# Sums of the latent heads in two bank pairs, value blocks inside the attention's first steps, front reordered, modulation rows turned by transposes

## The chip, the cores and the metric

The kernel is one program on one core of a Trainium2 chip. TensorE (PE) multiplies, VectorE (DVE), ScalarE (ACT) and GpSimd (POOL) work element by element, SyncE (SP) issues the transfers. The metric is the device time of one execution in microseconds; lower is better.

## The reference

Two transformer blocks of depth 2 run over 512 latent tokens (the first block also over 256 context tokens), width 1024. What matters here is the first layer of the first block:

```python
shift, scale, gate = modulation(c, ada_w[i], ada_b[i])      # silu(cond) @ ada_w + ada_b, for c and c_ctx
h = rms_norm(x, norm_g[i]) * (1 + scale) + shift
lat = split_cols(jnp.dot(h, w_in), EVEN_SPLITS)
q = jnp.dot(rms_norm(q_lat, q_norm), w_uq).reshape(bsz, n, A_HEADS, A_QK)       # 8 heads of 96
kv = jnp.dot(rms_norm(kv_lat, kv_norm), w_ukv).reshape(bsz, n, A_HEADS, A_NOPE + A_V)
q = rms_norm(q, q_gain)
k = rms_norm(k, k_gain)                                     # then a rotation of 32 of the 96 rows
a_x = block_attention(q_x, jnp.concatenate([k_x, k_c], axis=1), jnp.concatenate([v_x, v_c], axis=1), scale)
```

Beside this attention the layer has a gated linear attention ("gla") whose output is also normalized per head. The later layers are not touched, except that their modulation vectors are made by the same helper.

## The kernel before, in words

Each engine has its own hand-written instruction list; semaphores alone order them. Tokens lie along the free axis (768 = 512 + 256), so a result of 768 columns takes two PSUM banks. PSUM has 8 banks of 512 floats.

The front: SP issues `cond`, `vec`, the tokens and then the weights. `Modulation` k (twelve of them, classes START_MOD, GLA_MOD and LATE_MOD) multiplies the conditioning rows with four weight tiles (`pe`, L320), ACT copies the result out of PSUM (`copied`, L329), PE turns it into columns (`turned`, L336), DVE adds the bias (`added`, L343). DVE multiplies the tokens with the norm factor (L2816), makes the gains (L2806), ACT shifts and rounds (L2658, L2662), DVE takes the remainder (L2829). The first three weight tiles are split into a rounded part by ACT (`first_hi`, L522) and a remainder by POOL (`first_lo`, L527); `first_pe(t, h)` (L539 to L541) multiplies half h of tile t, four chunks of six matmuls.

The latent stage (class Latent): PE projects six query tiles (`q_tile`, L1118) and four key tiles (`k_tile`, L1134). For each of 20 heads (4 gla outputs, 8 query heads, 8 key heads) ACT squares (L1235), PE sums over the partitions into banks 4 and 5 (`sums`, L1154), ACT takes the logarithm out of PSUM (L1249) and the exponential (L1251), and DVE multiplies (`normed`, L1354). Query heads are also rotated (POOL L1347, DVE L1359, L1362), key heads are first taken from PSUM (DVE L1380). `sums(n)` waits on `hd_log` n, that is until ACT has read the sums of head n-1 out of the one pair of banks. Six value blocks (`value`, L1166, evicted by ACT L1305) follow among the last three heads' sums, into banks 0 to 3.

Then `att_mla` (class Pairs) runs its 24 steps: scores (L1929, banks 0 to 3), DVE maxima (L2028), ACT exponentials (L1994), PE turnings of the probabilities (L1942, banks 4 and 5), copies (L2003, L2049), values (L1956, bank 6). No engine begins it before all heads and all six value blocks are done (`latent.wait`).

## Time and profile before

| | us |
|---|---|
| median of 3 runs | 2326.94 |
| lowest, highest | 2325.99, 2331.77 |
| profiled execution | 2324.17 |
| its span in the profile | 2322.1 |
| PE busy | 2245.8 |
| DVE busy | 1144.2 |
| ACT busy | 981.6 |
| POOL busy | 371.4 |

The span is the part of the execution that the profile sees. PE is by far the busiest engine, so what moves the time is its idle time, the time in which it runs at the lower clock, and the instructions it executes.

### The profile page before, as it was taken

The page shows a single profiled execution, that of the slowest core. Times are in us where ns is not written, and L with a number is a line of the kernel's source. Part 1 is how long each engine was busy: PE and PEld are TensorE (multiplying, and loading weights), DVE is VectorE, ACT ScalarE, POOL GpSimd, SP SyncE. Part 2 cuts the span into 40 slices and gives each one's busy share as a digit, 9 for nine tenths or more (in the row PEclk, how much of TensorE's full clock was granted, in tenths as well). Part 3 has the DMA queues.
Part 4 walks back from the last instruction along what each step waited for, and adds up shares of the span by engine and source line. Part 5 has one row for each costly group of instructions (what it writes and reads, how often), then busy time and mean ns, then how long its engine had stood idle before and what let it go on. Part 6 is the DMA issues. An engine that isn't in the chain of part 4 may idle for free.

```text
span 2322.1 us, 32240 instructions
## 1 busy us (share of the span) xinstructions
PE 2245.8 (97%) x12310; PEld 1753.9 (76%) x12310; DVE 1144.2 (49%) x1778; ACT 981.6 (42%) x1642; POOL 371.4 (16%) x247
## 2 busy tenths in 40 slices
PE   6999999899999999999999999999999999999998
PEld 4888775366878877777876788888888667888886
DVE  5000453544353303754556476674555654766645
ACT  5121435645245524654256443342342764333422
POOL 2233001100323331030000300004300012000143
PEclk9999999899999999999999999999999999999999
DMA  8122241200132222124510323333344103333331
GB/s 328 46 64 64 82 168 25 76 34 1 47 117 73 66 80 78 56 85 118 141 55 4 97 91 94 97 90 100 93 130 131 37 23 96 91 96 94 92 99 46
DMA packets 58429, 197.72 MB, mean 85 GB/s; under 512 B 8059, under 2 KB 8443, under 8 KB 58044
## 3 DMA queue, kind: packets, MB, share of 16 engines
q1 hardware_dynamic: 58300, 195.94, 27.1%
q8 instruction: 89, 1.46, 0.2%
q14 instruction: 40, 0.33, 0.0%
HBM read 184.04 MB, written 2.10 MB: 80 GB/s over the span
## 4 chain that ended last, share of the span: by engine, by line
PE 89%; ACT 5%; DVE 4%; issue 1%; DMA 0%; POOL 0%; SPq 0%; DVEq 0%; ACTq 0%; POOLq 0%
PE PS L660 7%; PE PS L658 7%; PE PS L659 7%; PE PS L1929 4%; PE PS L2618 4%; PE PS L2620 3%; PE PS L2619 3%; PE PS L1956 3%; PE PS L1597 3%; PE PS L1942 3%; PE PS L610 3%; PE PS L611 3%; PE PS L609 3%; PE PS L854 2%; PE PS L856 2%; PE PS L855 2%
## 5 line engine op out<-in xcount | busy, mean ns | idle before, releaser
L658 PE MATMUL PS<-H_HI,W_SPLIT 128*128 128x512 f32 x672 | 265.5, 395 | 0.0
L660 PE MATMUL PS<-H_HI,W_SPLIT 128*128 128x512 f32 x672 | 264.9, 394 | 0.0
L659 PE MATMUL PS<-H_LO,W_SPLIT 128*128 128x512 f32 x672 | 264.5, 394 | 0.0
L504 POOL TENSOR_TENSOR W_SPLIT<-WT,W_SPLIT 128x1024 fp32r<-128x1024 f32 x43 | 104.6, 2434 | 612.8 <-ACT W_SPLIT L493 495.5
L470 ACT ACTIVATE W_SPLIT<-WT 128x1024 fp32r<-128x1024 f32 x80 | 84.8, 1060 | 267.3 <-PE PS L660 267.3
L2969 DVE TENSOR_TENSOR W_SPLIT<-WT,W_SPLIT 128x1024 fp32r<-128x1024 f32 x80 | 98.0, 1225 | 150.1 <-ACT W_SPLIT L470 150.0
L1062 POOL TENSOR_TENSOR OUT_HALF<-WT,OUT_HALF 128x512 fp32r<-128x512 f32 x48 | 71.3, 1487 | 610.0 <-ACT OUT_HALF L1020 610.0
L2955 DVE TENSOR_TENSOR G_LO<-SB,G_HI 128x512 fp32r<-128x512 f32 x43 | 100.4, 2335 | 109.0 <-ACT G_HI L2777 109.0
L659 PEld LDWEIGHTS PS<-H_LO,W_SPLIT 128*128 128x128 f32 x672 | 126.0, 188 | 30.4 <-issue 0.5
L658 PEld LDWEIGHTS PS<-H_HI,W_SPLIT 128*128 128x128 f32 x672 | 126.2, 188 | 29.9 <-issue 0.5
L660 PEld LDWEIGHTS PS<-H_HI,W_SPLIT 128*128 128x128 f32 x672 | 126.2, 188 | 29.8
L2618 PE MATMUL PS<-G_HI,W_SPLIT 128*128 128x512 f32 x344 | 135.7, 394 | 0.2
L2620 PE MATMUL PS<-G_HI,W_SPLIT 128*128 128x512 f32 x344 | 134.9, 392 | 0.0
L2619 PE MATMUL PS<-G_LO,W_SPLIT 128*128 128x512 f32 x344 | 133.5, 388 | 0.0
L611 PE MATMUL PS<-HN_HI,W_HALF 128*128 128x512 f32 x352 | 118.7, 337 | 0.0
L610 PE MATMUL PS<-HN_LO,W_HALF 128*128 128x512 f32 x352 | 118.7, 337 | 0.0
L609 PE MATMUL PS<-HN_HI,W_HALF 128*128 128x512 f32 x352 | 118.5, 337 | 0.0
L2039 DVE CUSTOM_DVE_ANT_0 SB<-PS,SB 128x512 f32<-128x512 f32 (+3 forms) x160 | 78.7, 527 | 68.9 <-PE PS L1929 65.5
L1805 POOL TENSOR_TENSOR W_HALF<-WT,W_HALF 128x512 fp32r<-128x512 f32 x60 | 82.5, 1376 | 164.4 <-ACT W_HALF L1634 164.4
L929 DVE TENSOR_TENSOR W_SPLIT<-WT,W_SPLIT 128x1024 fp32r<-128x1024 f32 x42 | 51.5, 1225 | 115.2 <-ACT W_SPLIT L891 115.2
L891 ACT ACTIVATE W_SPLIT<-WT 128x1024 fp32r<-128x1024 f32 x42 | 44.5, 1060 | 146.1 <-PE PS L856 98.7
L1942 PEld LDWEIGHTS PS<-SB 128*128 128x128 f32 x640 | 70.6, 142 | 45.3 <-issue 34.3
(353 smaller groups left out, 5257.9 us busy)
## 6 DMA issues: line engine op xcount, KB each, us to landing
WT<-weights SPq DMA_DIRECT2D x313, 512.0 KB, 3.6
SB<-SB SPq DMA_DIRECT2D x128, 64.0 KB
SB<-weights SPq DMA_DIRECT2D x13, 512.0 KB, 13.0
XT<-tokens SPq DMA_DIRECT2D x4, 768.0 KB, 7.2
SB<-rpb SPq DMA_DIRECT2D x8, 384.0 KB, 3.6
HT<-rpb SPq DMA_DIRECT2D x8, 384.0 KB, 3.7
out<-HT SPq DMA_DIRECT2D x4, 512.0 KB, 3.2
SB<-late SPq DMA_DIRECT2D x1, 1280.0 KB, 5.9
```

What stands on the lines that cost most here:

```text
L504: g.tensor_tensor(w[:, 1, :], W[:, (g0 + t) % SLOTS, :], w[:, 0, :].bitcast(F32), ALU.subtract).then_inc(sem("w_lo"), 1)
L609: pe.matmul(dst, hi, HN_HI[:, c, at:end], start=(c == 0), stop=False)
L610: pe.matmul(dst, hi, HN_LO[:, c, at:end], start=False, stop=False)
L611: last = pe.matmul(dst, lo, HN_HI[:, c, at:end], start=False, stop=(c == KC - 1))
L658: pe.matmul(PS[:, s, :], hi, H_HI[:, c, :], start=(c == 0), stop=False)
L659: pe.matmul(PS[:, s, :], hi, H_LO[:, c, :], start=False, stop=False)
L660: last = pe.matmul(PS[:, s, :], lo, H_HI[:, c, :], start=False, stop=(c == KC - 1))
L1942: last = pe.transpose(PS[:, 4 + k % 2, (b - b0) * 128:(b - b0) * 128 + 128], self.p(s, b // nb)[:, (b % nb) * 128:(b % nb) * 128 + 128], I ...
L2618: pe.matmul(PS[:, n, :], hi, ghi, start=first, stop=False)
L2619: pe.matmul(PS[:, n, :], hi, glo, start=False, stop=False)
L2620: last = pe.matmul(PS[:, n, :], lo, ghi, start=False, stop=(u == FC - 1))
L2955: v.tensor_tensor(lo, G[:, t, :], hi.bitcast(F32), ALU.subtract).then_inc(sem("g_lo"), 1)
```

## The change

- Sums: heads 4 to 19 use banks 4, 5 and 6, 7 in turn (`sum_bank`). `sums(n)` then waits for the logarithm of head n-2, not n-1.
- Values: blocks 0 to 2 follow the attention's first scores, blocks 3 to 5 the first step's turnings; they use banks 4 to 7. Their six evictions, and ACT's first split of the next weights (`window.out_hi`), move into ACT's first two attention steps. PE begins scores 0 without waiting for the value blocks.
- Modulation: `turned` is four transposes (128x128) in place of four matmuls with a 2-column selection; `added` is a sum over the four row groups out of PSUM and then the bias add. The identity matrix is loaded by itself between `vec` and the tokens.
- Front: remainders of tiles 1 and 2 are made by DVE, between its norm products; ACT splits the first half of tile 2 earlier; PE puts one chunk of tile 1 between the last modulation and its turning.

```diff
                 for b in range(4):
-                    last = pe.matmul(PS[:, self.turned_bank, 2 * b:2 * b + 2], self.row[:, b * 128:b * 128 + 128],
-                                     SB[:, vec_at + VEC["sel"]:vec_at + VEC["sel"] + 2], start=True, stop=True)
+                    last = pe.transpose(PS[:, self.turned_bank, 128 * b:128 * b + 128], self.row[:, b * 128:b * 128 + 128], IDENT)
...
-                v.tensor_tensor(MOD[:, self.chunk:self.chunk + 4, :], PS[:, self.turned_bank, 0:8].rearrange("p (c s) -> p c s", s=2),
-                                SB[:, at:at + 4].unsqueeze(2).broadcast_to([128, 4, 2]), ALU.add).then_inc(sem("mod_added"), 1)
+                mod = MOD[:, self.chunk:self.chunk + 4, :]
+                v.tensor_reduce(mod, PS[:, self.turned_bank, :].rearrange("p (c g s) -> p c s g", g=4, s=32)[:, :, 0:2, :], AX.X, ALU.add)\
+                 .then_inc(sem("mod_summed"), 1)
+                v.wait_ge(sem("mod_summed"), self.k + 1)
+                v.tensor_tensor(mod, mod, SB[:, at:at + 4].unsqueeze(2).broadcast_to([128, 4, 2]), ALU.add).then_inc(sem("mod_added"), 1)
...
+            def sum_bank(self, n):
+
+                return 6 if n >= 4 and n % 2 else 4
+
             def sums(self, pe, n):
                 _, parts, _ = self.head(n)
                 pe.wait_ge(sem("hd_squared"), n + 1)
-                if n >= 1:
+                if n == 5:
+                    pe.wait_ge(sem("kv_log"), 2)
+                elif n >= 6:
+                    pe.wait_ge(sem("hd_log"), n - 1)
+                elif n >= 1:
                     pe.wait_ge(sem("hd_log"), n)
...
+            def first_values(self, pe, att):
+
+                pe.wait_ge(sem("k_out"), 8)
+                pe.wait_ge(sem("hd_done"), 2)
+                pe.wait_ge(sem("hd_normed"), 14)
+                att.scores(pe, 0)
+                for b in range(3):
+                    self.value(pe, b)
+
+            def late_values(self, pe):
+                for b in range(3, 6):
+                    self.value(pe, b)
+
+            def values_out(self, act, s):
+
+                if s < 2:
+                    for b in range(3 * s, 3 * s + 3):
+                        self.value_out(act, b)
+                if s == 1:
+                    window.out_hi(act, 0, 0)
+                    window.out_hi(act, 0, 1)
...
             sp.dma_start(SB[:, vec_at:vec_at + NVEC], vec).then_inc(sem("vec_in"), 16)
+            sp.dma_start(IDENT, con[:, 0:128]).then_inc(sem("vec_in"), 16)
...
             START_MOD[2].turned(pe)
             START_MOD[3].pe(pe)
+            first_pe(pe, 1, 0, [0])
             START_MOD[3].turned(pe)
-            first_pe(pe, 1, 0)
+            first_pe(pe, 1, 0, [1, 2, 3])
             first_pe(pe, 2, 0)
...
                     v.tensor_tensor(H[:, c, :], X[:, c, :], RS0, ALU.mult).then_inc(sem("normed"), 1)
-                START_MOD[2 * part].added(v)
+                    if c == 5:
+                        START_MOD[2].added(v)
+                        v.wait_ge(sem("half_lo"), 2)
+                        first_lo(v, 1, 0)
+                        first_lo(v, 1, 1)
+                if part:
+                    first_lo(v, 2, 0)
+                else:
+                    START_MOD[0].added(v)
```

The first place is PE's front, from the last modulation on (L320 is its multiplication, L336 the turning, L539 to L541 and in the changed kernel L542 to L544 the first tiles). Before:

```order
L320 MATMUL PS<-WT,SB 32x512 [waits w_ready7]
L320 MATMUL PS<-WT,SB 32x512
L336 MATMUL PS<-SB 128x2 [waits mod_added,ada_copied]
L336 MATMUL PS<-SB 128x2 x3
L539 MATMUL PS<-HN_HI,W_FIRST 128x512 [waits half_lo]
```

The same place of the changed kernel:

```order
L320 MATMUL PS<-WT,SB 32x512 [waits w_ready7]
L320 MATMUL PS<-WT,SB 32x512
L542 MATMUL PS<-HN_HI,W_FIRST 128x512 [waits half_lo]
L543 MATMUL PS<-HN_LO,W_FIRST 128x512
L544 MATMUL PS<-HN_HI,W_FIRST 128x512
L542 MATMUL PS<-HN_HI,W_FIRST 128x256
L543 MATMUL PS<-HN_LO,W_FIRST 128x256
L544 MATMUL PS<-HN_HI,W_FIRST 128x256
L336 MATMUL PS<-SB 128x128 [waits mod_added,ada_copied]
L336 MATMUL PS<-SB 128x128 x3
```

One chunk now stands ahead of the turning, and the turning is four transposes.

The second place is DVE's front, the second half of the norm products (L2859 in the changed kernel; L529 is the remainder, L343 the sum out of PSUM, L346 the bias, L2849 the gain):

```order
L2859 TENSOR_TENSOR HT<-XT,SB 128x768 x2
L343 TENSOR_REDUCE SB<-PS 128x8 [waits ada_turned]
L346 TENSOR_TENSOR SB<-SB 128x8 [waits mod_summed]
L529 TENSOR_TENSOR W_FIRST<-SB,W_FIRST 128x512 [waits half_hi,half_lo]
L529 TENSOR_TENSOR W_FIRST<-SB,W_FIRST 128x512 [waits half_hi]
L2859 TENSOR_TENSOR HT<-XT,SB 128x768 x2
L529 TENSOR_TENSOR W_FIRST<-SB,W_FIRST 128x512 [waits half_hi]
L343 TENSOR_REDUCE SB<-PS 128x8 [waits ada_turned]
L346 TENSOR_TENSOR SB<-SB 128x8 [waits mod_summed]
L2849 SCALAR_TENSOR_TENSOR SB<-SB 128x8 [waits mod_added]
L529 TENSOR_TENSOR W_FIRST<-SB,W_FIRST 128x512 [waits half_hi]
```

Before, four norm products stood together, then both bias adds and the gain, and the four remainders were POOL's.

The third place is PE's end of the latent stage (L1154 sums, L1166 a value block, L1929 scores). Before, from the value blocks after the last sums on:

```order
L1166 MATMUL PS<-WT,SB 128x512 x4
L1166 MATMUL PS<-WT,SB 128x512 [waits v_out1]
L1166 MATMUL PS<-WT,SB 128x512
L1166 MATMUL PS<-WT,SB 128x512 [waits v_out1]
L1166 MATMUL PS<-WT,SB 128x512
L1929 MATMUL PS<-SB,HT 128x256 [waits v_out1,hd_normed,hd_done]
L1929 MATMUL PS<-SB,HT 128x256
L1929 MATMUL PS<-SB,HT 128x512 x2
L1929 MATMUL PS<-SB,HT 128x256 [waits at_exped] x2
```

The changed kernel (L1169 sums, L1187 a value block, L1963 scores), from the last sums on:

```order
L1169 MATMUL PS<-SB 96x512 [waits hd_log,hd_squared]
L1169 MATMUL PS<-SB 96x256
L1963 MATMUL PS<-SB,HT 128x256 [waits hd_normed,hd_done,k_out]
L1963 MATMUL PS<-SB,HT 128x256
L1963 MATMUL PS<-SB,HT 128x512 x2
L1187 MATMUL PS<-WT,SB 128x512 [waits hd_log,w_ready6]
L1187 MATMUL PS<-WT,SB 128x512 x3
L1187 MATMUL PS<-WT,SB 128x512 [waits hd_log]
L1187 MATMUL PS<-WT,SB 128x512
L1963 MATMUL PS<-SB,HT 128x256 [waits at_exped,hd_normed,hd_done]
```

The first scores moved ahead of the value blocks, and three blocks stand between the scores of steps 0 and 1; the other three (not shown) stand behind the first step's turnings.

## Rows read from the trace of the kernel before

**Rows 1.** The page, busy time, share of the span and instructions of each engine.

```profile
PE 2245.8 (97%) x12310; PEld 1753.9 (76%) x12310; DVE 1144.2 (49%) x1778; ACT 981.6 (42%) x1642; POOL 371.4 (16%) x247
```

**Rows 2.** Waits of PE over the span: total us, times, longest.

```profile
PE PS L1154 <- ACT SB L1249: 8.9, 7, 2.0
```

**Rows 3.** Timeline, SP, front: start us, us, engine, line, count.

```profile
1.67 1.91 SPq L2367 DMA_DIRECT2D XT<-tokens  x4
```

**Rows 4.** Timeline, PE, front; in brackets the idle time before and who ended it.

```profile
39.00 1.92 PE L320 MATMUL PS<-WT,SB 128*32 128x512 f32 x16
...
42.29 1.02 PE L336 MATMUL PS<-SB 128*128 128x2 f32 x8 [1.37 <-DVE SB L343]
...
53.17 0.40 PE L539 MATMUL PS<-HN_HI,W_FIRST 128*128 128x512 f32 x1
...
54.22 0.39 PE L539 MATMUL PS<-HN_HI,W_FIRST 128*128 128x512 f32 x1
```

**Rows 5.** Stretch 44 to 48: busy time of each engine, clock share, DMA.

```profile
44.00:48.00 4.00, 4.00 (x17) 3.47 (x16) 2.75 (x5) 3.11 (x4) 0.70 (x1) 0.60 1.03 410
```

**Rows 6.** Timeline, DVE and POOL, front.

```profile
32.29 0.96 DVE L2829 TENSOR_TENSOR HN_LO<-HT,HN_HI 128x768 fp32r<-128x768 f32 x1 [0.30 <-ACT HN_HI L2662]
...
36.33 5.73 DVE L2816 TENSOR_TENSOR HT<-XT,SB 128x768 f32<-128x768 f32 x4
36.50 3.88 POOL L527 TENSOR_TENSOR W_FIRST<-SB,W_FIRST 128x512 fp32r<-128x512 f32 x2 [7.64 <-ACT W_FIRST L522]
...
41.99 0.15 DVE L343 TENSOR_TENSOR SB<-PS,SB 128x8 f32<-128x8 f32 x1
...
43.55 1.18 DVE L2806 SCALAR_TENSOR_TENSOR SB<-SB 128x8 f32<-128x8 f32 x1
```

**Rows 7.** Timeline, PE, gla stage: eight transposes, a turning.

```profile
260.18 1.04 PE L2497 MATMUL PS<-SB 128*128 128x128 f32 x8
...
283.77 1.05 PE L336 MATMUL PS<-SB 128*128 128x2 f32 x8
```

**Rows 8.** Timeline, PE, latent stage and the attention's start.

```profile
382.91 7.90 PE L1118 MATMUL PS<-SB,WT 128*128 128x512 f32 x24
390.65 1.46 PE L1154 MATMUL PS<-SB 97*96 97x512 f32 x4
...
416.32 1.50 PE L1154 MATMUL PS<-SB 96*96 96x512 f32 x4 [1.99 <-ACT SB L1249]
417.65 2.75 PE L1134 MATMUL PS<-SB,WT 128*128 128x512 f32 x8
...
439.72 5.30 PE L1166 MATMUL PS<-WT,SB 128*128 128x512 f32 x8
...
446.15 7.03 PE L1166 MATMUL PS<-WT,SB 128*128 128x512 f32 x16
454.15 2.82 PE L1929 MATMUL PS<-SB,HT 96*128 96x256 f32 x8 [0.96 <-ACT SB L1305]
...
468.86 1.04 PE L1942 MATMUL PS<-SB 128*128 128x128 f32 x8
...
470.80 1.53 PE L1956 MATMUL PS<-SB 128*64 128x128 f32 x24
```

**Rows 9.** Timeline, ACT: logarithms of two heads, a value eviction, copies.

```profile
429.55 0.88 ACT L1249 ACTIVATE SB<-PS,SB 96x768 f32<-96x768 f32 x1
...
432.12 0.90 ACT L1249 ACTIVATE SB<-PS,SB 96x768 f32<-96x768 f32 x1
...
443.35 0.78 ACT L1305 ACTIVATE SB<-PS,SB 128x512 f32<-128x512 f32 x1 [1.52 <-PE PS L1166]
...
463.70 1.09 ACT L2003 ACTIVATE SB<-PS 128x512 f32<-128x512 f32 x2 [4.59 <-PE PS L1942]
```

**Rows 10.** Stretches 429 to 433 and 433 to 443, columns as in rows 5.

```profile
429.00:433.00 4.00, 1.50 (x4) 0.57 (x4) 3.25 (x4) 3.97 (x5) 0.00 (x0) 0.99 0.00 0
433.00:443.00 10.00, 8.76 (x12) 3.61 (x13) 4.43 (x5) 6.08 (x8) 0.00 (x0) 0.50 0.00 0
```

More of the change, by code:

```diff
@@ L523, in first_hi, with first_lo, first_pe @@
                .then_inc(sem("half_hi"), 1)
-        def first_lo(g, t, h):
-            g.wait_ge(sem("half_hi"), 2 * t + h + 1)
-            g.tensor_tensor(W_FIRST[:, t, 1, h * 512:h * 512 + 512], RAW[:, 8 + t, h * 512:h * 512 + 512],
+        def first_lo(eng, t, h):
+            eng.wait_ge(sem("half_hi"), 2 * t + h + 1)
+            eng.tensor_tensor(W_FIRST[:, t, 1, h * 512:h * 512 + 512], RAW[:, 8 + t, h * 512:h * 512 + 512],
                             W_FIRST[:, t, 0, h * 512:h * 512 + 512].bitcast(F32), ALU.subtract).then_inc(sem("half_lo"), 1)
-        def first_pe(pe, t, h):
+        def first_pe(pe, t, h, chunks=None):
             pe.wait_ge(sem("half_lo"), 2 * t + h + 1)
-            for c in range(4 * h, 4 * h + 4):
+            chunks = range(4 * h, 4 * h + 4) if chunks is None else chunks
+            for c in chunks:
                 if t == 0:
@@ L541, in first_pe @@
                     last = pe.matmul(dst, lo, HN_HI[:, c, at:end], start=False, stop=(c == KC - 1))
-            last.then_inc(sem("ev_early" if h else "half_used"), 1)
+            if chunks[-1] == 4 * h + 3:
+                last.then_inc(sem("ev_early" if h else "half_used"), 1)
         def split_halves_act(act, name, n, take, last=True):
@@ L1151, in sums, with value_bank @@
                     deep = 97
-                    pe.wait_ge(sem("lat_eps"), 2)
+                    pe.wait_ge(sem("lat_rows"), 3)
                 for b, lo, hi in halves(N):
-                    last = pe.matmul(PS[0:parts, 4 + b, 0:hi - lo], ONES[0:deep, 0:parts], self.SQ[0:deep, n % 2, lo:hi],
+                    last = pe.matmul(PS[0:parts, self.sum_bank(n) + b, 0:hi - lo], ONES[0:deep, 0:parts], self.SQ[0:deep, n % 2, lo:hi],
                                      start=True, stop=True)
                 last.then_inc(sem("hd_summed"), 1)
+            def value_bank(self, b):
+                return (4, 5, 6, 7, 6, 7)[b]
             def value(self, pe, b):
@@ L1161, in value @@
                     pe.wait_ge(sem(f"w_ready{t % SLOTS}"), (t // SLOTS + 1) * 16)
-                    pe.wait_ge(sem("k_out"), 8)
+                    pe.wait_ge(sem("hd_log"), 19)
+                if b == 2:
+                    pe.wait_ge(sem("hd_log"), 20)
                 if b >= 4:
-                    pe.wait_ge(sem("v_out1"), b - 3)
+                    pe.wait_ge(sem("v_out1"), b - 1)
                 for c in range(2):
-                    last = pe.matmul(PS[:, b % 4, :], self.KVL[:, c, b * 128:b * 128 + 128], W[:, t % SLOTS, c * 512:c * 512 + 512],
+                    last = pe.matmul(PS[:, self.value_bank(b), :], self.KVL[:, c, b * 128:b * 128 + 128], W[:, t % SLOTS, c * 512:c * 512 + 512],
                                      start=(c == 0), stop=(c == 1))
@@ L1190, in pe @@
                 last.then_inc(sem("lat_summed"), 1)
-                for h in range(17):
+                for h in range(16):
                     if h in (1, 2, 4):
@@ L1195, in pe @@
                         self.k_tile(pe, (h - 5) // 2)
-                    if h < 16:
-                        self.sums(pe, 4 + h)
-                    if h >= 14:
-                        self.value(pe, 2 * (h - 14))
-                        self.value(pe, 2 * (h - 14) + 1)
+                    self.sums(pe, 4 + h)
+            def first_values(self, pe, att):
[15 more added lines that the diff above has]
+                    window.out_hi(act, 0, 1)
             def lat_square(self, act, c):
@@ L1248, in factor @@
                     eps, scale, unit = EPSV[0:parts, 7:8], 1.0 / parts / UNIT_K, EPSV[0:parts, 10:11]
-                act.activation(rs, self.wide(4, parts), ACT.Ln, bias=eps, scale=scale).then_inc(sem("hd_log"), 1)
+                act.activation(rs, self.wide(self.sum_bank(n), parts), ACT.Ln, bias=eps, scale=scale).then_inc(sem("hd_log"), 1)
                 act.wait_ge(sem("hd_log"), n + 1)
@@ L1304, in value_out @@
                 act.wait_ge(sem("kv_rs"), 2)
-                act.activation(V1[:, b, :], PS[:, b % 4, :], ACT.Identity, bias=NIL, scale=self.RC[:, b:b + 1]).then_inc(sem("v_out1"), 1)
+                act.activation(V1[:, b, :], PS[:, self.value_bank(b), :], ACT.Identity, bias=NIL, scale=self.RC[:, b:b + 1]).then_inc(sem("v_out1"), 1)
             def swap(self, sp, dst, src, signal):
@@ L2588, in _ @@
             latent.pe(pe)
+            latent.first_values(pe, att_mla)
             latent.wait(pe)
@@ L3159 @@
     put("subln", a["odd_subln_2"])
-    for g in range(4):
-        vec[32 * g, VEC["sel"]] = vec[32 * g + 1, VEC["sel"] + 1] = 1.0
     put("conv_w", a["ffn_conv_w_2"].reshape(2, 3, 2, FC, 128).transpose(0, 1, 3, 2, 4))
```

48 lines of the change are left out of this document (27 added, 21 removed).

## The prediction

> **What bounds the kernel now.** I read the page first: PE is busy 2245.8 of 2322.1 us [rows 1], so 76 us of idle time, its slow-clock time and its own instructions are all there is to win. The list of waits comes second, because it says where that idle time lies: the largest entry that this change touches is the sums L1154 waiting for the logarithm L1249, 8.9 us in 7 waits [rows 2]. Then I read PE's timeline at the three places that the diff touches, and the stretches for the clock. The reader is to see three things. In the front PE idles 1.37 us ahead of a turning, for a DVE add that stands behind four norm products [rows 4]. In the gla stage PE runs without a gap, so there each instruction saved counts in full. In the latent stage PE waits for ACT, and the clock is at its lower level (1.2 GHz) from 433 to 443, after a stretch of 4 us in which PE worked 1.50 [rows 10].
>
> **Latent stage and the attention's start.** I take the time from the sums of head 6 (390.65) to the first values of the attention (470.80) [rows 8]: 80.15 us before. The changed order issues exactly the same PE work in it:
> - sums of heads 6 to 19: 14 times 1.3 (416.32 to 417.65 is one) = 18.2
> - the last query tile: 390.65 - 382.91 = 7.7
> - four key tiles: 4 times 2.6 (the row's 2.75 without its last matmul's drain) = 10.4
> - six value blocks: 7.03 / 4 = 1.75 each = 10.5
> - scores of steps 0 to 2: 2.7 each (2.82 with the last one's drain) = 8.1
> - turnings of two steps: 470.80 - 468.86 = 1.9 each = 3.9
>
> That is 58.8 us; the other 21.4 are waits and slow clock [rows 8]. What stays of them? ACT needs 432.12 - 429.55 = 2.57 us for a head (logarithm, exponential, square) [rows 9]. For heads 12 to 15 PE has half a key tile beside each sum and takes 2.6, so both are even; for heads 16 to 19 PE has 1.3 only and waits 1.27 each, 5.1 in all. At the first key heads ACT's square waits for DVE's product of a key tile, and for head 12 there is a second square: about 2.1 at head 12 and 1.2 at head 14, which two banks don't remove. Sum 8.4. The waits before heads 7, 10, 17 and the like, where PE only waited for the one bank pair, go. The value blocks cover what was open from 456.97 on: step 1's scores no longer wait for step 0's maximum and exponential, since three blocks (5.3 us) lie between, and step 2's have three more. ACT gets six evictions (0.78 each, as before) into the first two steps, in the second of which it idled 4.59 us ahead of a copy [rows 9]; the first three fall while PE is on value blocks. So at full clock the stage takes 58.8 + 8.4 = 67.2.
>
> The clock is the unknown. Before, ten microseconds at 1.2 GHz [rows 10] made two value blocks cost 5.30 and not 3.5 [rows 8], and two sums twice their 1.3. In the changed kernel heads 16 to 19 keep PE at 1.3 of 2.6 us, more sparsely than anywhere before, so I expect the lower level to come again. But a sum at 1.2 GHz takes 2.6, which fits under ACT's 2.57 with two banks (before, sum and logarithm followed each other), so only scores and value blocks behind it pay, about 2 us. Bounds: 0, and 5 if the ten microseconds lie wholly on dense work. Term: 80.15 - 67.2 - 2 = **-11.0** (-8 to -13).
>
> **Gla stage.** A turning now is eight passes for four matmuls and takes 1.05; eight transposes take 1.04, so four take half of it [rows 7], a little over it with the drain of the last, and I take 0.46 as saved. Six turnings stand in a stretch without PE idle: 6 times 0.46 = **-2.8**. No row shows DVE's new sum of 32 strided PSUM elements; the nearest is the bias add out of PSUM at 0.15 [rows 6], and with the add and the semaphore between I take +0.3 per modulation. It is not on PE's path: before such a step DVE waits for PE, and PE asks for the add only one modulation later. Bounds for this term: -2.8, and 0 if DVE's longer step came to bind.
> A transpose's row shows 0.27 us while its neighbours start every 0.13 [rows 7]. The Trainium skill, TensorE: Matmul & The Clock Gate, section Part 4: PE-mode transpose, gives about 275 ns for one in a kernel. By that figure an estimate for a turning would be 1.1 us, and all twelve would cost 1.5 us more and not less; the trace has the same duration, but shows that they overlap.
>
> **Front.** From the last modulation (39.00) to the second half of tile 0 (53.17) before: 14.17 us [rows 4]. Work in it: 1.9 for L320, the turning, and eight chunks of 1.05 (54.22 - 53.17) [rows 4]; about 1.7 us went to the lower clock around 44 to 48, where PE was busy all the time at a share of 0.60 [rows 5], and 1.37 to the wait. In the new order: 1.9 + 1.05 + 0.5 + 7 times 1.05 = 10.8 if nothing waits. DVE's side: four norm products took 5.73 while POOL ran its remainders; one such operation with POOL quiet takes 0.96 [rows 6]. So products 4 and 5 end 1.9 us after 36.33, the add of modulation 2 waits for its turning (about 38.8), two remainders at 0.65 (two thirds of 0.96) end at about 40.5, ahead of the chunk (40.7 at the earliest); products 6 and 7 and the third remainder end near 43, the adds and the gain near 43.8, where before the gain ended at 44.73 [rows 6]. The new remainder behind the gain costs ACT 0.3. PE asks for the remainder of chunk 4 at about 49.8; after a gain at 43.8 its shift, rounding and remainder, each under 1 us, are done by 47: no wait. With no idle PE the clock should hold; if not, 1.7 is lost. Saved: 3.4, plus 0.45 for turning 2, minus what the identity costs: its issue (0.47, a quarter of 1.91 [rows 3] with the gap) stands ahead of the tokens and everything up to PE's start hangs on the transfers; 64 KB at the 410 GB/s of [rows 5] is 0.16. I take 0.4. The two longer adds in the first half stand where the gain waits for POOL's remainder anyway. Term: **-3.4** (-0.5 to -4).
> The gain of 8 columns took 1.18 and ended with POOL's remainder; without POOL it is a matter of 0.2 [rows 6]. The Trainium skill, SBUF — State Buffer, section SBUF: two separate sides, says why: VectorE and GpSimd share one pair of ports under an exclusive lock, for the whole instruction. The trace agrees (1.43 us for a product of 0.96).
>
> **Late modulations** (two): PE waits there for DVE's remainders, not for the turning. 0, up to +0.5 for the longer adds.
>
> **Sum.** -11.0 - 2.8 - 3.4 = -17.2. Against the profiled execution, 2324.17, it gives 2307.0. The median of the runs shown, 2326.94, is 2.8 above that execution, so the changed kernel's median should be **2310**.
>
> **Rivals.**
> - *The sum holds*, 2304 to 2316: chance 0.78.
> - *The clock eats half of it.* With heads 12 to 19 PE works half the time, from 412 on; if the lower level begins there and lies on the key tiles (10.4), all three score steps and the values, 18 us of work take 9 more: -8, 2319. For it: rows 10 show the fall after just such a stretch. Against: around 412 to 416 before, PE also idled 1.99 us and kept its clock. Chance 0.10.
> - *ACT becomes the bound of the attention's start.* Its six evictions and the weight split come before its copies and exponentials of steps 1 and 2. If all 4.7 us of the evictions showed up as delay, -12.5 would be left; if the chunk in the front also waited for DVE (3.4 lost), -9.1, and with the clock at its worse bound (3 more) -6: 2321, no change that can be told. Against: ACT idled 4.59 us at this place [rows 9]. Chance 0.08.
> - *Slower.* The lower clock stays through the attention's 24 steps: about 85 us of PE time, of which more than half is work. From 17 us of PE work at 1.2 GHz on, the sum is used up; with 40 us the time is 2350. Rows show that dense work ended each spell so far. Chance 0.04.
>
> **The numbers.** A measurement tells about 0.3% (7 us) from no change: faster is below 2320. Faster has the first two cases, 0.88; the third is same, 0.08; slower 0.04. The range takes the first case and most of the second, and its low end adds the full-clock bounds (-13, -2.8, -4 give 2307 by the median; a lower median of the runs, 2 less): 2304 to 2319.
>
> **What would show it.** Right: PE's list of waits has the sums waiting for squares and not for logarithms, about 5 waits of 1.3 at the last four heads; the scores of step 1 start without a wait; turnings 0.5 apart from the next work; PE without a gap from 39 to 53, first half-1 chunk near 50. Wrong: waits of the attention's first turnings or values for ACT's evictions; a clock share of 0.5 over more than ten microseconds after head 12; the chunk before turning 3 waiting for DVE.

## The result, and the profile after

The changed kernel takes 2308.81 us (median of 6 runs, 2306.38 to 2312.62), beside 2327.11 for the kernel before (6 runs on the same chip): a ratio of 0.9929, with a 95% interval from 0.9914 to 0.9945. The same file timed later on another chip gave 0.9921 (0.9907 to 0.9934). The forecast was 2310, within 2304 to 2319. The profiled execution took 2306.38 (forecast 2307.0) with a span of 2304.4.

The page's busy line and PE's waits of the kernel after answer to [rows 1] and [rows 2] (L1169 are the heads' sums, L1274 the squares, L1288 the logarithms):

```profile
PE 2232.2 (97%) x12262; PEld 1742.3 (76%) x12262; DVE 1145.2 (50%) x1794; ACT 980.9 (43%) x1642; POOL 364.7 (16%) x243
...
PE PS L1169 <- ACT SB L1274: 6.9, 5, 2.4
...
PE PS L1169 <- ACT SB L1288: 1.2, 2, 1.1
```

PE is busy 13.6 us less and idle some 4 us less. The sums wait for squares now, 6.9 us in 5 waits, where they waited 8.9 us in 7 for logarithms. PE's timeline at the front answers to [rows 4] (L542 are the early chunks):

```profile
38.94 0.60 PE L336 MATMUL PS<-SB 128*128 128x128 f32 x4
39.47 1.92 PE L320 MATMUL PS<-WT,SB 128*32 128x512 f32 x16
41.32 0.50 PE L542 MATMUL PS<-HN_HI,W_FIRST 128*128 128x512 f32 x1
...
42.48 0.60 PE L336 MATMUL PS<-SB 128*128 128x128 f32 x4
...
50.26 0.39 PE L542 MATMUL PS<-HN_HI,W_FIRST 128*128 128x512 f32 x1
```

No row has a wait in brackets: from the last modulation to the second half of tile 0 it is 50.26 - 39.47 = 10.79 us, where it was 14.17. PE's timeline from head 6's sums to the first values (L1990) answers to [rows 8]:

```profile
385.76 2.75 PE L1169 MATMUL PS<-SB 97*96 97x512 f32 x8
...
408.93 2.58 PE L1169 MATMUL PS<-SB 96*96 96x512 f32 x4 [2.35 <-ACT SB L1274]
...
423.20 1.53 PE L1169 MATMUL PS<-SB 96*96 96x512 f32 x4 [1.67 <-ACT SB L1274]
425.69 1.53 PE L1169 MATMUL PS<-SB 96*96 96x512 f32 x4 [0.96 <-ACT SB L1274]
...
432.03 2.74 PE L1963 MATMUL PS<-SB,HT 96*128 96x256 f32 x8
434.61 5.31 PE L1187 MATMUL PS<-WT,SB 128*128 128x512 f32 x12
439.76 2.75 PE L1963 MATMUL PS<-SB,HT 96*128 96x256 f32 x8
...
453.86 1.53 PE L1990 MATMUL PS<-SB 128*64 128x128 f32 x24
```

This stretch, "the stage" from here on, takes 453.86 - 385.76 = 68.10 us, where it took 80.15. Step 1's scores (439.76) start behind the value blocks without a wait.

Where the time went, as the shift of like rows against the kernel before: the gla stage's first turn 253.55 to 250.64, -2.91; the gla stage (from that turn to the first query tile) 84.94 to 82.96, -1.98; the latent part up to head 6's sums 52.16 in both; the stage -12.05. That is -16.94; the later stages are 0.8 shorter, and the span is 17.7 shorter.

### The profile page after: what moved, and what is told of

Its sections match the earlier page's. It is cut to its first block, busy times and chain, and to the rows that moved or that the text cites. A ratio compares the mean times of both kernels' runs of the same rounds, so it can differ in the third digit from the quotient of the medians.

```text
span 2304.4 us, 32161 instructions
## 1 busy us (share of the span) xinstructions
PE 2232.2 (97%) x12262; PEld 1742.3 (76%) x12262; DVE 1145.2 (50%) x1794; ACT 980.9 (43%) x1642; POOL 364.7 (16%) x243
## 4 chain that ended last, share of the span: by engine, by line
PE 89%; ACT 5%; DVE 4%; issue 1%; DMA 0%; POOL 0%; SPq 0%; DVEq 0%; ACTq 0%; POOLq 0%
PE PS L667 7%; PE PS L665 7%; PE PS L666 7%; PE PS L1963 4%; PE PS L2663 4%; PE PS L2665 4%; PE PS L2664 3%; PE PS L1990 3%; PE PS L1630 3%; PE PS L1976 3%; PE PS L617 3%; PE PS L618 3%; PE PS L616 3%; PE PS L861 2%; PE PS L863 2%; PE PS L862 2%
```

## The experiments

All of them in one table: the first square of ACT (it waits for the tokens), PE's start, the gla stage's first turn and the gla stage's length, the stage, each from one profiled execution; then the median and the ratio to the kernel before, timed on the same chip in 5 rounds. Chips differ (the kernel before had medians from 2323.4 to 2327.3), so compare ratios across groups. Groups timed on one chip each: (1) the kernel after; (2) sums_only to turn_undone; (3) ident_in_before to k_early; (4) after_again to dve_order; (5) order_and_fill.

| kernel | square | PE | turn | gla | stage | median | ratio (95%) |
|---|---|---|---|---|---|---|---|
| before | 6.41 | 13.95 | 253.55 | 84.94 | 80.15 | 2327.11 | 1 |
| after | 8.54 | 15.49 | 250.64 | 82.96 | 68.10 | 2308.81 | 0.9929 (0.9914-0.9945) |
| sums_only | 7.79 | 14.87 | 249.69 | 82.96 | 75.47 | 2312.43 | 0.9949 (0.9934-0.9963) |
| values_only | 8.36 | 15.29 | 250.11 | 82.96 | 71.16 | 2313.30 | 0.9952 (0.9937-0.9967) |
| front_undone | 7.72 | 14.77 | 255.04 | 84.58 | 71.70 | 2314.70 | 0.9956 (0.9941-0.9972) |
| turn_undone | 6.40 | 13.88 | 248.59 | 84.94 | 68.68 | 2309.62 | 0.9941 (0.9923-0.9958) |
| ident_in_before | 7.92 | 14.85 | 253.13 | 86.06 | 80.12 | 2325.92 | 1.0002 (0.9993-1.0012) |
| ident_late | 6.42 | 13.66 | 248.37 | 84.58 | 68.66 | 2306.07 | 0.9920 (0.9906-0.9934) |
| front_sel | 7.74 | 15.01 | 251.57 | 82.96 | 71.00 | 2310.51 | 0.9933 (0.9920-0.9947) |
| k_early | 8.69 | 15.63 | 250.61 | 82.96 | 70.52 | 2308.78 | 0.9929 (0.9915-0.9942) |
| after_again | 7.96 | 14.92 | 249.61 | 84.58 | 71.64 | 2308.50 | 0.9921 (0.9907-0.9934) |
| pe_fill | 7.67 | 15.12 | 249.83 | 84.54 | 68.44 | 2307.91 | 0.9919 (0.9906-0.9933) |
| dve_order | 6.26 | 13.37 | 248.34 | 82.96 | 67.18 | 2305.70 | 0.9911 (0.9898-0.9925) |
| order_and_fill | 6.48 | 13.82 | 249.50 | 82.96 | 66.53 | 2305.49 | 0.9917 (0.9905-0.9930) |

**What one execution can tell: after_again.** Nothing is edited; it stands first because the others can't be read without it.

> The changed kernel once more, nothing altered. It shows what a single profiled execution can tell: the kernels so far, alike in the front up to PE's start, started PE between 13.66 and 15.63 us, and the spells at the lower clock lay at different places. Theory (both are chance of the execution): start, first turn of the gla stage and stage of the latent part differ from 15.49, 250.64 and 68.10 by up to 1 to 2 us each, with no edit to account for it, and the spells of 408 to 413 and of about 1870 move or are missing. Rival (both follow from the kernel): the same numbers within 0.3 us and the same spells.

The first theory holds, and the stage goes beyond its numbers. PE started 0.57 earlier, the first turn came 1.03 earlier, the gla stage took 1.62 more and the stage 3.54 more, in the same program; the spell of 1870 is missing. The stretches of the two profiles show what differs (column behind POOL's: the granted clock), first the kernel after, then the same kernel again:

```profile
254.00:256.00 2.00, 2.00 (x16) 1.67 (x15) 0.00 (x0) 1.41 (x1) 0.00 (x0) 1.00 0.02 6
...
410.00:412.00 2.00, 2.00 (x4) 0.96 (x3) 1.93 (x3) 1.96 (x3) 1.23 (x1) 0.50 0.13 25
...
430.00:432.00 2.00, 1.34 (x4) 0.76 (x5) 0.92 (x1) 1.97 (x3) 0.00 (x0) 1.00 0.00 0
```

```profile
254.00:256.00 2.00, 2.00 (x12) 2.00 (x11) 0.00 (x0) 1.97 (x2) 0.00 (x0) 0.50 0.00 0
...
410.00:412.00 2.00, 2.00 (x5) 1.03 (x4) 1.86 (x3) 1.94 (x3) 0.63 (x1) 0.63 0.09 16
...
430.00:432.00 2.00, 2.00 (x5) 0.68 (x4) 0.91 (x1) 1.84 (x4) 0.00 (x0) 0.50 0.00 0
```

A spell at 1.2 GHz (0.50) lay at 253 to 257 and from 424 to 438 in the second execution and not in the first; the one at 410 came in both. So a difference of 1.6 in the gla stage or of up to 3.5 in the stage, between two single profiles, may be a spell. What stands below rests on waits and on stretches at the full clock; the medians average over the spells.

**The stage: banks or value blocks? sums_only, values_only.** The first puts the value blocks back, the second the single pair of banks:

```diff
 # sums_only: as in the kernel before
-                return (4, 5, 6, 7, 6, 7)[b]
+                return b % 4
...
-                    pe.wait_ge(sem("hd_log"), 19)
...
+                    pe.wait_ge(sem("k_out"), 8)
...
+                    if h >= 14:
+                        self.value(pe, 2 * (h - 14))
+                        self.value(pe, 2 * (h - 14) + 1)
...
-                        dve_takes=(2,), scored_ahead=1, projected=latent)
+                        dve_takes=(2,))
...
 # values_only
-                return 6 if n >= 4 and n % 2 else 4
+                return 4
...
```

> The changed kernel with its value blocks put back where they were (two beside each of the last two heads' sums, two behind them, evictions between the heads' factors); the sums still go to two pairs of banks in turn. Stage from the sums of head 6 to the attention's first values: 80.15 us before, 68.10 changed. Theory (the two parts share the gain): the waits of the sums for logarithms go, but the attention's start again waits for maxima and exponentials and runs partly at the lower clock: stage 73 to 76 us, time 2314 to 2317. Rival (the value blocks carry it all, since the heads are paced by ACT and DVE with one pair of banks as with two): stage 79 to 80, time about 2320. Rival 2 (the banks carry it): stage 69, time 2310.

> The changed kernel with all sums in one pair of banks (each waits for the logarithm of the head before it), the value blocks inside the attention's first two steps. Theory (shared gain): PE's sums wait for logarithms again, 7 to 9 us in 7 waits, of which about half only takes the place of the waits for squares: stage 72 to 74 us, time 2313 to 2315. Rival (value blocks carry it all): stage 69, time 2310. Rival 2 (the banks carry it): stage 79, time about 2320.

PE's timeline of sums_only (L1971 scores, L1998 values), then of values_only (L1165 sums, L1984 values):

```profile
384.82 2.74 PE L1169 MATMUL PS<-SB 97*96 97x512 f32 x8
...
443.60 2.82 PE L1971 MATMUL PS<-SB,HT 96*128 96x256 f32 x8 [0.96 <-ACT SB L1346]
447.73 0.70 PE L1971 MATMUL PS<-SB,HT 96*128 96x256 f32 x2 [1.32 <-ACT SB L2042]
...
460.29 1.53 PE L1998 MATMUL PS<-SB 128*64 128x128 f32 x24
```

```profile
385.23 1.46 PE L1165 MATMUL PS<-SB 97*96 97x512 f32 x4
...
425.49 1.50 PE L1165 MATMUL PS<-SB 96*96 96x512 f32 x4 [1.08 <-ACT SB L1282]
428.07 1.50 PE L1165 MATMUL PS<-SB 96*96 96x512 f32 x4 [1.08 <-ACT SB L1282]
...
456.39 1.53 PE L1984 MATMUL PS<-SB 128*64 128x128 f32 x24
```

With the value blocks back the attention's start waits again: 0.96 for the last eviction and 1.32 for step 0's exponential. With one pair of banks the last sums come every 2.58 (428.07 - 425.49), and with two every 2.48, so there the second pair saves only 0.1 a head; its gain lies in the earlier heads, whose waits come back (8.6 us for logarithms in 8 waits in the whole span of values_only, and 2.4 in two more, ahead of the sums of heads 7 and 10, for which the profile names no releaser). In the profiles sums_only gives back 7.4 of the 12.05 and values_only 3.1, a little less than theory one's range for the latter. The medians (2312.43 and 2313.30, same chip) don't show that difference; by the ratios each gives back 4.6 to 7 us. Some 2.8 of the 7.4 is clock: a spell from 425 to 432 lay on two of the value blocks (4.58 us for two, where two take 3.5 at full clock), and another from 448 to 453 on scores (4.11 for six matmuls that take 2.42 at full clock further on). values_only had one spell in the stage, at 411 to 416, as the kernel after has one at 409 to 413, so its 3.1 isn't clock; beside after_again's 71.64 its stage alone would tell nothing. So both parts carry the gain, and neither rival, under which one part carries it all, stands.

**The front's order: front_undone.** The diff's front part reversed (POOL's remainders, chunks, copies), transposes kept:

```diff
-                        if 8 * q + s == 0:
-                            first_lo(g, 0, h)
+                        first_lo(g, 8 * q + s, h)
                         continue
...
-            first_pe(pe, 1, 0, [0])
             START_MOD[3].turned(pe)
-            first_pe(pe, 1, 0, [1, 2, 3])
+            first_pe(pe, 1, 0)
...
-                    if c == 5:
-                        START_MOD[2].added(v)
...
```

> The changed kernel with the front's order as before (POOL makes all six early remainders, all four chunks of tile 1 behind turning 3, tile 2's first half copied behind modulation 3's row); transposed turnings and the identity's load stay. First turn of the gla stage: 253.55 us before, 250.64 changed. Theory: the order alone is worth more than the -2.9 that the front shows, since the identity's load took about 1.3 of it: the first turn comes at 254 to 255 and the time is 2312 to 2313. Rival (the lower clock from 44 to 48 was all that the order removed): it comes at about 252.5, time 2310.5.

The first turn came at 255.04, 4.4 later, and the ratio is up by 6 us: the theory's side, and beyond its numbers (of the 6 us, spells in the gla stage and the latent stage have a share: 84.58 and 71.70 in the table). The timeline of front_undone shows why (POOL's L529 are the remainders, DVE's L343 the reduction of the turned row, L346 the bias add):

```profile
42.44 3.03 POOL L529 TENSOR_TENSOR W_FIRST<-SB,W_FIRST 128x512 fp32r<-128x512 f32 x2 [0.99 <-ACT W_FIRST L524]
43.06 0.18 DVE L343 TENSOR_REDUCE SB<-PS 128x8 f32<-128x32 f32 x1
43.27 1.01 DVE L346 TENSOR_TENSOR SB<-SB 128x8 f32<-128x8 f32 x1
...
44.42 1.09 PE L336 MATMUL PS<-SB 128*128 128x128 f32 x4 [3.27 <-DVE SB L346]
```

The wait ahead of turning 3 is 3.27, where it was 1.37 [rows 4]. DVE reads the turned row out of PSUM in 0.18 with POOL at work, but the new bias add from SBUF to SBUF takes 1.01. So the transposed turnings with their load would have made the front later in the old order too: 255.04 beside 253.55, that is 1.5, where in the new order it is 2.05 (turn_undone, next). Two such differences between single profiles can't be told apart, so nothing here shows that the two edits depend on each other. The order by itself brings the first turn 4.4 to 5.0 earlier. The spell at the lower clock around 44 to 48 [rows 5] stands in all three profiles with the old order (before, ident_in_before, front_undone) and in none of the eleven with the new one, so its going belongs to the order and isn't chance.

**The turnings: turn_undone.** Selecting columns again, and no early load:

```diff
-                    last = pe.transpose(PS[:, self.turned_bank, 128 * b:128 * b + 128], self.row[:, b * 128:b * 128 + 128], IDENT)
+                    last = pe.matmul(PS[:, self.turned_bank, 2 * b:2 * b + 2], self.row[:, b * 128:b * 128 + 128],
+                                     SB[:, vec_at + VEC["sel"]:vec_at + VEC["sel"] + 2], start=True, stop=True)
...
-            sp.dma_start(IDENT, con[:, 0:128]).then_inc(sem("vec_in"), 16)
```

> The changed kernel with turnings by eight matmuls against two selecting columns and one bias add out of PSUM, without the identity's early load; front order and latent stage as changed. Theory: PE's first matmul goes back from 15.49 us to 14.0, the first turn of the gla stage comes 0.5 to 1 earlier than 250.64 (1.3 to 1.5 from the load, less 0.4 for each of the turnings 2 and 3), the gla stage is 2.0 longer (84.9), so the time is 1 to 1.5 longer: 2310. Rival (the load costs nothing and the later start has another cause): the start stays at 15.5, the first turn comes at 251.4 and the time is 2311.6.

The gla stage took 84.94, to the hundredth what it took before, so the -1.98 there is all the turnings'. But the first turn came at 248.59, 2.05 earlier than with them. This part of the change gives back in the front what it gains in the gla stage: spans 2303.6 and 2304.4, and a ratio that can't be told from the changed kernel's. The front loses more than the load: in the kernel after, DVE's two bias adds of the first half also stand beside POOL:

```profile
26.66 3.31 POOL L529 TENSOR_TENSOR W_FIRST<-SB,W_FIRST 128x512 fp32r<-128x512 f32 x2 [25.35 <-ACT W_FIRST L524]
27.54 0.18 DVE L343 TENSOR_REDUCE SB<-PS 128x8 f32<-128x32 f32 x1
27.75 1.02 DVE L346 TENSOR_TENSOR SB<-SB 128x8 f32<-128x8 f32 x1
...
28.91 1.09 DVE L346 TENSOR_TENSOR SB<-SB 128x8 f32<-128x8 f32 x1
...
43.65 0.17 DVE L346 TENSOR_TENSOR SB<-SB 128x8 f32<-128x8 f32 x1
```

and PE's first chunk waits 1.3 for what follows, where turn_undone's starts without a wait. From DVE's first norm product to its first remainder for that chunk it is 7.95 to 8.11 us in the ten profiles with transposed turnings in the front and 7.03 to 7.61 in the four with selected columns. The Trainium skill, SBUF — State Buffer, section SBUF: two separate sides, has a VectorE operation with two inputs in SBUF and a GpSimd operation that reads SBUF take one pair of ports in turn, each for the whole instruction. By that rule an add whose two inputs lie in SBUF waits until POOL's operation is over; the trace agrees (1.02 and 1.09 here, the second ending at 30.00 where POOL's ends at 29.97, and 0.17 for the same add at 43.65, when POOL is idle).

**The identity's load: ident_in_before, ident_late, front_sel.** The load alone added to the kernel before; the changed kernel with it behind eight weight tiles; the changed kernel with the first four turnings by selecting columns and no early load.

```diff
 # ident_late
...
-            sp.dma_start(IDENT, con[:, 0:128]).then_inc(sem("vec_in"), 16)
...
                 sp.dma_start(RAW[:, k, :], weights[TILES + k]).then_inc(sem(f"raw_in{k}"), 16)
+                if k == 7:
+                    sp.dma_start(IDENT, con[:, 0:128]).then_inc(sem("con_in"), 16)
...
-            pe.wait_ge(sem("vec_in"), 32)
+            pe.wait_ge(sem("con_in"), 16)
```

> The kernel before with one thing added: the 64 KB load of the identity, ahead of the tokens, with DVE's and PE's first waits covering it. Theory (the load is what makes the start late): ACT's first square comes about 2 us later than 6.41, PE's first matmul at 15.4 to 15.9 and not 13.95, the first turn of the gla stage 1.3 to 1.6 later than 253.55, time 1.5 more than before. Rival (my forecast's 0.4): PE starts at 14.4 and the first turn comes 0.4 later.

> The changed kernel with the identity's load behind the eight weight tiles of modulations 0 and 1 and on a semaphore of its own, which PE waits for ahead of turning 0 only. Theory (position of the load): PE starts at 13.9 to 14.4 and not 15.49, the first turn of the gla stage comes at 249.3 to 249.8 and not 250.64, about 1 less than the changed kernel. Rival (the load only moves its own cost: PE waits for it at turning 0): first turn at 250.6 or later, same time.

> The changed kernel with the turnings of modulations 0 to 3 by matmuls against two selecting columns, as before, and those of 4 to 11 by transposes; no early load of the identity. With every turning by matmuls the first turn of the gla stage came at 248.59, with every one by transposes at 250.64. Theory (the load and the add that POOL's remainders hold up both belong to the front's turnings): first turn at 248.6, gla stage of 83.0 as in the changed kernel, in sum 2 less than the changed kernel: profiled time 2303 to 2304.5. Rival (the gla stage's saving needs something of the front): first turn at 248.6 but the gla stage 84.9, no gain.

ACT's first square, which waits for the tokens, in the kernel after and in front_sel (the others are in the table):

```profile
8.54 1.57 ACT L2692 ACTIVATE HT<-XT 128x768 f32<-128x768 f32 x2 [3.97 <-DMA XT<-tokens]
```

```profile
7.74 1.58 ACT L2699 ACTIVATE HT<-XT 128x768 f32<-128x768 f32 x2 [3.00 <-DMA XT<-tokens]
```

The last one has no early load and is late all the same, so this too is partly chance. Over the table's profiles: with the load ahead of the tokens the first square comes at 7.72 to 8.69 (7 profiles, PE's start 15.12 on average); without it five times at 6.26 to 6.48 and twice at 7.7 (front_sel, pe_fill; mean start 14.12). The load costs about 1.0 us of PE's start on average, not 0.4. In time this is little: ident_in_before has a ratio of 1.0002 (0.9993 to 1.0012), and I can't tell 1 us from nothing there. Neither of its expectations was met: PE's start, 14.85, lies between the two, and the first turn came 0.4 earlier than in the kernel before, not later. The kernel before had a spell from 33 to 37 that cost its early chunks 0.5, and ident_in_before has none there. In ident_late the first turn came 2.3 earlier than in the kernel after, more than expected, and a spell at 252 to 257 took 1.6 of it back. front_sel's gla stage is 82.96, as its first theory said, but its first turn came at 251.57 and not at 248.6: tokens that came late and a spell from 34 to 38 hid the gain at the front, so that this run decides nothing on time.

**Who paces the heads: k_early, dve_order.** My forecast had ACT's pace and saw waits of about 2.1 at head 12 and 1.2 at head 14. DVE is busy 1.83 to 1.94 of each 2 us from 404 to 424 in the kernel after. First DVE's key products one head earlier, then its last four rotations later as well (with the late load):

```diff
 # k_early
-                    if h in (6, 8, 10, 12):
-                        p = (h - 6) // 2
+                    if h in (5, 7, 9, 11):
+                        p = (h - 5) // 2
 # dve_order also
-                    if 2 <= h < 10:
+                    if 2 <= h < 6:
                         self.roped(v, h - 2)
+                    if h >= 12:
+                        self.roped(v, h - 8)
```

> The changed kernel with DVE's products of each key tile one head earlier in DVE's order (ahead of the normalization of heads 9, 11, 13, 15 and not 10, 12, 14, 16). Theory: ACT's squares of heads 12, 14, 16 and 18 stand in wait for these products behind DVE's other work, so PE's wait of 2.35 ahead of head 12's sums goes and that of 1.67 ahead of head 16's shrinks to about 1: the stage from head 6's sums to the first values goes from 68.10 to 65 to 66, time 2 to 3 less. Rival (DVE is saturated from 404 to 424, at 1.9 of each 2 us, so its order cannot matter): the wait at head 12 only moves to heads 14 and 16, the stage stays within 0.7 of 68.1.

> The kernel with the late identity load, DVE's products of each key tile one head earlier, and its last four rotations (1.36 us of two operations each) moved from behind the normalizations of heads 10 to 13 to behind those of heads 16 to 19, where DVE idled 0.7 to 1.5 us a head. Theory (DVE's load, not the order alone, sets the pace of heads 12 to 16; with the products earlier alone the sums of head 16 came 2.8 earlier and head 19's not at all): the waits at heads 12 and 16 shrink from 2.35 and 1.67 to under 1, ACT's 2.5 a head sets the pace throughout, the sums of head 19 come 2.5 to 4 earlier: stage from head 6's sums to the first values 64.5 to 66.5 at full clock, up to 3 more if scores or value blocks fall into a spell. Rival (the rotations moved back come to bind: step 1's scores wait for the last of them): a new wait of 1 to 2 at those scores, stage 67 to 68.

PE's timeline of k_early, then of dve_order (L1965 scores):

```profile
407.55 1.53 PE L1169 MATMUL PS<-SB 96*96 96x512 f32 x4 [1.00 <-ACT SB L1274]
...
424.22 8.44 PE L1169 MATMUL PS<-SB 96*96 96x512 f32 x12 [2.26 <-ACT SB L1274]
432.45 4.71 PE L1963 MATMUL PS<-SB,HT 96*128 96x256 f32 x8
```

```profile
424.30 2.88 PE L1169 MATMUL PS<-SB 96*96 96x512 f32 x4 [0.95 <-ACT SB L1274]
426.97 4.58 PE L1965 MATMUL PS<-SB,HT 96*128 96x256 f32 x8
```

k_early shortens the wait at head 12 to 1.00, but one of 2.26 stands at head 17, and the scores start at 432.45, not earlier than in the kernel after (432.03): the rival holds, though a spell over the last three sums took its share of that. With less DVE work in the way, dve_order starts head 19's sums 40.84 us behind head 6's (424.30 - 383.46), where the kernel after takes 44.90: 4.1 saved, and DVE's load is thereby shown as what paced heads 12 to 16. A spell then made the sums 2.67 and the scores 4.42, 3.1 more than at full clock, so only 0.9 of the 4.1 reached this profile's stage. dve_order has the lowest ratio, 0.9911; timed beside after_again (2305.8 to 2309.8), four of its five runs (2304.22 to 2306.51) lie below the other's fastest. It also has the late load, and the interval of its ratio and that of ident_late (0.9920) overlap by most of their width, so how much of the time is the order's isn't shown.

**Can the clock be held? pe_fill, order_and_fill.** Matmuls that nobody reads, in PE's waits, on the base of ident_late and of dve_order:

```diff
+                if n == 12 or n >= 16:
+                    pe.wait_ge(sem("hd_log"), n - 1)
+                    for w in ((512, 512) if n == 12 else (512, 256) if n == 16 else (512,)):
+                        pe.matmul(PS[:, self.sum_bank(n), 0:w], ONES, self.KVL[:, 0, 0:w], start=True, stop=True)
                 pe.wait_ge(sem("hd_squared"), n + 1)
```

> The kernel with the late identity load, and in PE's waits ahead of the sums of heads 12 and 16 to 19 matmuls whose results nobody reads (512 columns each, two at head 12, one and a half at head 16), into the bank that the sums overwrite. Without them PE ran at 1.2 GHz for most of 409 to 416 and of 422 to 431, and its stage from head 6's sums to the first values was 68.66. Theory (the lower clock follows PE's idle stretches, and at the sums it costs nothing since ACT sets the pace there): both spells go; the spell of 409 to 416 had slowed two key tiles' work, so the stage is 67.0 to 67.5, 1.2 to 1.7 less, no more, and the waits for squares turn into busy time. Rival (spells come whatever PE does in these waits): they stay, and each added matmul at the lower clock takes 1.7 and not 0.86, so the sums fall behind ACT: stage 70 to 73.

> The kernel with the late identity load and DVE's new order, and unread matmuls in PE's waits where that kernel had them: 512 columns ahead of the sums of heads 12, 18 and 19, 256 ahead of head 14's, 768 ahead of head 17's. Without them a spell at 1.2 GHz from 423 to 431 made head 19's sums take 2.67 and not 1.3 and step 0's scores 4.42 and not 2.6, in a stage of 67.18. Theory (the spell follows the sparse stretch ahead of it, and costs only where PE has dense work): filled, the spell goes or moves, the stage is 63.8 to 64.6 and the kernel's time 2302 to 2305. Rival (with the waits filled a spell comes elsewhere in the stage, at the key tiles, as from 416 to 422 in the filled kernel before): stage 65.5 to 67.2, time no other than 2305.7.

Stretches of ident_late and then of pe_fill:

```profile
416.00:422.00 6.00, 4.86 (x16) 2.45 (x14) 5.63 (x8) 4.06 (x6) 0.00 (x0) 1.00 0.13 53
422.00:431.00 9.00, 7.90 (x13) 2.91 (x14) 6.50 (x7) 8.43 (x11) 0.00 (x0) 0.62 0.00 0
```

```profile
416.00:422.00 6.00, 5.08 (x10) 2.56 (x11) 5.66 (x7) 5.13 (x6) 0.35 (x1) 0.72 0.31 89
422.00:431.00 9.00, 9.00 (x28) 4.68 (x27) 6.88 (x8) 7.69 (x10) 0.00 (x0) 1.00 0.00 0
```

In pe_fill the spell of 422 to 431 is gone and one of 417 to 421 has come, behind a wait of 1.80 that wasn't filled; the stage is 68.44 for 68.66, and neither expectation is met in full. order_and_fill had every wait ahead of the sums filled, and no spell in the stage. But it won no more than 0.65 on dve_order's stage (66.53), because something else was next. PE's row of step 1's scores and DVE's rows ahead of it (L1401 the last rotation, L2077 step 0's maxima):

```profile
436.58 3.21 PE L1970 MATMUL PS<-SB,HT 96*128 96x256 f32 x8 [1.86 <-ACT SB L2041]
```

```profile
433.66 0.68 DVE L1401 TENSOR_TENSOR HT<-SB 32x512 f32<-32x512 f32 x1
434.37 1.82 DVE L2077 TENSOR_REDUCE SB<-PS 128x1 f32<-128x768 f32 x2
```

The rotations that were moved back hold up step 0's maxima, these ACT's exponential, and that step 1's scores. It is the rival of dve_order, which the slow scores had covered there. I had foreseen 63.8 to 64.6; with the 1.86 gone it would be 64.7 (an estimate, 66.53 - 1.86). The time (2305.49, ratio 0.9917) is dve_order's within what can be told. One execution without a spell doesn't prove that filling does it.

## Why the forecast was right, step by step

- **Latent stage, -11.0 (-8 to -13).** It came to -12.05, and in the second profile of the same kernel to -8.5. Six profiles have this latent stage unchanged (after, after_again, front_undone, turn_undone, ident_late, front_sel): 68.10 to 71.70, mean 69.96, so -10.2, and the profile that the forecast is held against is the shortest of them. The mechanism stands: no wait for logarithms at the late heads, step 1's scores behind value blocks, evictions that hold nobody up. Two steps of the working were wrong and partly cancelled. I took PE and ACT as even at heads 12 to 15; dve_order shows that DVE paced these. And I took 1.27 for each of four waits at the end, where one was 1.67 and three 0.95: ACT's period is 2.49, not 2.57. The waits for squares sum to 6.9, forecast 8.4.
- **"A sum at 1.2 GHz fits under ACT's pace, so only scores and value blocks pay, about 2 us."** Shown in both halves. In ident_late a spell from 423 to 431 lay on the sums and the scores still started 46.83 behind head 6's sums (kernel after: 46.27); in after_again a spell lay on sums and scores, and the stage was 3.5 longer. In the profiled execution of the changed kernel the spell came at 410 instead.
- **Gla stage, -2.8.** Mis-sized: -1.98. A turning saves 0.40 and not 0.46, and only five of the six save anything. The last one, in the kernel before and then after (L2547 and L2591 are PE's next matmuls):

```profile
335.04 1.05 PE L336 MATMUL PS<-SB 128*128 128x2 f32 x8
336.05 0.68 PE L2547 MATMUL PS<-SB,HT 128*128 128x128 f32 x4
```

```profile
330.14 0.66 PE L336 MATMUL PS<-SB 128*128 128x128 f32 x4
331.16 0.68 PE L2591 MATMUL PS<-SB,HT 128*128 128x128 f32 x4 [0.36 <-DVE SB L2929]
```

```profile
330.26 0.75 DVE L2929 TENSOR_TENSOR SB<-SB,PS 128x256 f32<-128x256 f32 x2 [1.17 <-PE PS L2597]
330.93 0.18 DVE L343 TENSOR_REDUCE SB<-PS 128x8 f32<-128x32 f32 x1
```

  It is 1.01 us from this turning to the next matmul before and 1.02 after: PE's next matmul needs DVE's addition of outputs (L2929), which the longer turning had covered. DVE's new reduction (L343) stands behind that addition, so the longer step that the term's upper bound had named is not what binds; the failed step is "Six turnings stand in a stretch without PE idle", counted in full: behind the last of them a wait was only hidden.
- **Front, -3.4.** It came to -2.9; five profiles with this front (after, sums_only, values_only, k_early, after_again) have a mean first turn of 250.13, so -3.4. The total was met by luck, since, as far as single profiles tell, two sizes were wrong and cancelled: the order brings the first turn 4.4 to 5.0 earlier and not 3.4, and the turnings with their load make it 1.5 to 2.05 later, where I had about nothing (0.4 less 0.45). The dense part was forecast as 10.8 and took 10.79. Up to the last modulation (39.00 before, 39.47 after) I had -0.05 and it came to +0.47: the first chunk +1.31 (33.12, behind a wait of 1.30), turning 2 -0.35, and -0.49 that is chance, the spell from 33 to 37 in the profile before, which ident_in_before hasn't. The failed steps are "I take 0.4" for the identity (about 1.0 on average and 1.5 in this pair of profiles) and "The two longer adds in the first half stand where the gain waits for POOL's remainder anyway", which held only in part: they took 1.02 and 1.09 themselves, and the gain behind them 0.17 where it had taken 0.97.
- **Rivals.** No wait of PE ends with one of ACT's evictions in the kernel after. The clock did not stay down through the attention's steps. Spells did eat some 3 us in single executions, less than the rival's 9. That 9 was too small for the rival's own words: the key tiles and three score steps alone are 18.5 us of work (10.4 + 8.1), and at half the clock they take as much again (a score step 4.40 beside 2.74 in after_again and after). The last rival's "about 85 us of PE time" is also too little: from 471 to 586 of the kernel before PE was busy 104 us.
- **A transpose's 275 ns.** The estimate of 1.1 us for a turning would make twelve 0.6 us dearer by the row's 1.05, not 1.5. Nothing rests on it: four transposes took 0.58 to PE's next instruction.
- **The sum** was 0.5 off because the stage's luck (-1.05 beyond forecast) covered the front and the gla stage (+1.3), and the later stages were 0.8 shorter (before had a spell at 665 to 669 that the changed kernel's profile hasn't). The median lies 2.4 above the profiled execution, where I had added 2.8. A forecast of each part to the microsecond from one profile isn't to be had here.

What stays open: whether the transposed turnings pay at all with the early load (the spans differ by 0.8, and the ratios 0.9929 and 0.9941 by less than their intervals), and how much of ident_late's 0.9920 is the load's place and how much chance. With the late load the transposes show no loss at the front (first turn 248.37 in ident_late, 248.59 in turn_undone), from one profile each. A kernel with dve_order's order but the last rotation behind step 0's maxima wasn't tried.

## What to carry to other kernels

Before you cost one add at nothing, look which engines read and write SBUF at that moment: an operation that moves from a PSUM operand to SBUF alone can cost six times as much beside POOL (1.02 for 0.17 here), and the delay shows at whatever waits next: ahead of turning 3 in one order, ahead of the first chunk in the other. Before you count a shortened instruction in full, look what it had covered: the last turning of the gla stage saved nothing. When a wait names the engine that released it, ask who had held that engine up; here "waits for ACT's square" meant DVE's load. And profile the same kernel twice before you read a difference of under 4 us out of one profile: match spells of the clock first, then waits, and only then durations. Where several kernels share a stage, average it over their profiles.

## What the runs showed of the hardware

- The same program has its spells at 1.2 GHz at different places from one execution to the next, each some 3 to 14 us long; on sums that ACT paces they cost nothing (ident_late), on scores or value blocks up to 3 us. The one at 253 to 257 in after_again began although PE had been idle for only 0.46 since 246.
- The tokens' arrival varies by 1.3 us with the same order of loads (first square at 6.4 or 7.7); a 64 KB load ahead of them moved it by 1.4 on average.
- Four transposes of 128x128 take 0.58 from one issue to the next instruction of PE (280.86 to 281.44), eight matmul passes for two columns 0.98.
